# SSD stage: one running-sums matmul per head, diagonal blocks clipped by ScalarE, z and values in two PSUM banks each

## The reference

```python
proj = h @ w_in[i]
z, xbc, dt_raw, q_a, kv_a, k_rope_raw, gates = jnp.split(proj, [...], axis=-1)
...
dt = jax.nn.softplus(dt_raw + dt_bias)
a = -jnp.exp(a_log)
# y_t = sum_{s<=t} (C_t . B_s) exp(sum_{s<k<=t} a_k) x_s dt_s
y = ssd_chunked_scan(xs * dt[..., None], dt * a, bm, cm)
y = y + xs * d_skip[:, None]
y = y.reshape(b, l, D_INNER) * jax.nn.silu(z)
```

## Time and profile before

| | us |
|---|---|
| median of 3 runs | 1741.97 (1741.3 to 1747.82) |
| the profiled execution | 1743.19 |
| its span | 1741.4 |
| PE busy in the span | 1678.2 |
| ACT busy in the span | 739.3 |
| DVE busy in the span | 1092.7 |

### The profile page before, as it was taken

How to read it: one execution, slowest core, us unless ns; L and a number is a source line. 1 busy time by engine, 2 the same in 40 slices (tenths; PEclk the granted TensorE clock), 3 DMA queues, 4 the chain that set the end, 5 groups by cost and what they waited for, 6 DMA issues and landing times.

```text
span 1741.4 us, 19963 instructions
## 1 busy us (share of the span) xinstructions
PE 1678.2 (96%) x7783; PEld 1326.5 (76%) x7783; DVE 1092.7 (63%) x1397; ACT 739.3 (42%) x1040; POOL 65.8 (4%) x90
## 2 busy tenths in 40 slices
PE   5999989999999999998999999998999999999998
PEld 2888767888888887885666788875668888888887
DVE  3788856532454567876767855546868796652364
ACT  3433413221222245558776323537842354441241
POOL 0005000000000000000000000001310000000000
PEclk9999998999999999999999999998999999999999
DMA  9454321222222232221111222220012222222222
GB/s 383 173 197 171 121 94 56 97 97 98 95 96 98 97 141 73 97 97 49 49 49 53 75 93 93 89 99 25 1 64 106 97 97 97 97 97 97 97 97 97
DMA packets 25422, 174.18 MB, mean 100 GB/s; under 512 B 2800, under 2 KB 3184, under 8 KB 5104
## 3 DMA queue, kind: packets, MB, share of 16 engines
q1 hardware_dynamic: 21440, 146.52, 23.5%
q10 hardware_dynamic: 3888, 26.38, 3.8%
HBM read 168.69 MB, written 4.19 MB: 99 GB/s over the span
## 4 chain that ended last, share of the span: by engine, by line
PE 79%; DVE 11%; ACT 6%; issue 2%; DMA 2%; ACTq 0%; DVEq 0%
PE bank L1512 24%; PE bank L1514 24%; PE bank L1513 24%; ACT p L378 2%; DVE w_lo L852 2%; DMA ada_chunk<-ada 2%; ACT pt L378 1%; DVE p L1260 1%; PE bank L2022 1%; PE bank L1877 1%; PE bank L1711 1%; PE bank L1693 1%; DVE rs_g L1284 1%; PE bank L1997 1%; ACT w_hi L378 1%
## 5 line engine op out<-in xcount | busy, mean ns | idle before, releaser
L1512 PE MATMUL bank<-h,w_hi 128*128 128x512 f32 x1200 | 478.3, 399 | 15.0 <-DVE zt L1226 5.0
L1514 PE MATMUL bank<-h,w_lo 128*128 128x512 f32 x1200 | 471.2, 393 | 0.0
L1513 PE MATMUL bank<-h,w_hi 128*128 128x512 f32 x1200 | 471.0, 393 | 0.0
L378 ACT ACTIVATE w_hi<-raw 128x2048 fp32r<-128x2048 f32 (+1 forms) x129 | 246.5, 1911 | 333.6 <-DMA raw<-slabs 329.2
L852 DVE TENSOR_TENSOR w_lo<-raw,w_hi 128x2048 fp32r<-128x2048 f32 (+1 forms) x129 | 294.6, 2284 | 103.0 <-ACT w_hi L378 99.2
L1512 PEld LDWEIGHTS bank<-h,w_hi 128*128 128x128 f32 x1200 | 227.7, 190 | 67.5 <-issue 18.4
L1513 PEld LDWEIGHTS bank<-h,w_hi 128*128 128x128 f32 x1200 | 227.6, 190 | 47.8 <-issue 1.2
L1514 PEld LDWEIGHTS bank<-h,w_lo 128*128 128x128 f32 x1200 | 227.5, 190 | 47.8
L1512 PE MATMUL bank<-a_hi,w_hi 128*128 128x512 f32 x432 | 168.4, 390 | 1.7 <-DVE a_lo L858 1.7
L1514 PE MATMUL bank<-a_hi,w_lo 128*128 128x512 f32 x432 | 168.3, 390 | 0.0
L1513 PE MATMUL bank<-a_lo,w_hi 128*128 128x512 f32 x432 | 168.3, 390 | 0.0
(11 more groups left out here) (340 smaller groups left out, 2264.0 us busy)
## 6 DMA issues: line engine op xcount, KB each, us to landing
raw<-slabs SPq DMA_DIRECT2D x127, 1024.0 KB, 4.8
ada_chunk<-ada ACTq DMA_DIRECT2D x24, 1024.0 KB, 7.3
x<-x_in SPq DMA_DIRECT2D x4, 1024.0 KB, 8.8
spill_x<-x SPq DMA_DIRECT2D x1, 2048.0 KB, 12.0
x<-spill_x SPq DMA_DIRECT2D x2, 1024.0 KB, 6.6
out<-x SPq DMA_DIRECT2D x8, 256.0 KB, 2.0
raw<-slabs SPq DMA_DIRECT2D x2, 768.0 KB, 4.3
inv<-inv ACTq DMA_DIRECT2D x1, 1024.0 KB, 6.9
```

Of the source, the lines that this page charges most:

```text
L378: return act.activation(out, in_, f, **kw)
L1512: pe.matmul(out, w[0], a[0], start=start, stop=False)
L1513: pe.matmul(out, w[0], a[1], start=False, stop=False)
L1514: return pe.matmul(out, w[1], a[0], start=False, stop=stop)
```

## The change

- `running_sums` issues one matmul a head, over all 512 columns, into one bank (3 or 4). The mask matmul and its wait for the mask ahead of the stage are gone. It waits for a new signal `row_used` instead of `e2_made`; `row_used` is told when ACT has read the bank for the last time.
- ACT writes, in the place of the four exponentials of the diagonal blocks, the positive part of acum_s - acum_t (Relu with scale -1 and the new column `acum_col` as bias). The other three exponentials read the same bank. Then two more activations take exp(-value) in place in `p2`, each over two diagonal blocks of 128 columns. Above the diagonals this gives 1, and `sm` is zero there. The wait for the buffer `p2[hd % 4]` is one wait for a whole earlier pair's values instead of one for each block row.
- `acum_col` is copied once from bank 4, at xbc tile 3, into memory that the spill of x has freed.
- z alternates between banks 0 and 5, the values between 6 and 7. z tiles wait for the gate two pairs back, values for `ys_made` two pairs back. The wait of the values for `s2_taken` is as it was.
- The first group's scores come behind z tile 0, not ahead of the first running sums.

The diff, whole:

```diff
--- before.py
+++ after.py
@@ -178,6 +178,7 @@
     acum = at("acum", [S], f32, A + 97 * K)
     acum_parts = at("acum_parts", [S], f32r, A + 103 * K)
     nac_col = at("nac_col", [TOK, SSD_H], f32, A + 105 * K)
+    acum_col = at("acum_col", [TOK, SSD_H], f32, 15 * K)
     dt_col = at("dt_col", [TOK, SSD_H], f32, A + 105 * K + 512)
     rope = at("rope", [2, TOK, ROPE // 2], f32, A + 105 * K)
     qk_g = at("qk_g", [2, QK], f32, A + 104 * K)
@@ -301,7 +302,7 @@
 
     up_banks = [(first_banks, banks[0:2], banks[6:8])[n % 3] for n in range(SLABS["upa"])] + [banks[0:2]] * SLABS["upb"]
 
-    near_banks, far_banks = [banks[n] for n in (5, 7)], [banks[n] for n in (3, 4)]
+    sum_banks, z_banks, value_banks = [banks[n] for n in (3, 4)], [banks[n] for n in (0, 5)], [banks[n] for n in (6, 7)]
 
     unit_banks = [(banks[0], banks[1]), (banks[4], banks[5])]
 
@@ -635,6 +636,8 @@
                     act.wait_ge(sem("dt_turned"), 1)
                     for first, place in ((0, nac_col), (P, dt_col)):
                         do(fn(place[:], banks[4][:, first:first + P].rearrange("p (t g) -> p t g", t=TOK), ACT.Copy))
+                    act.wait_ge(sem("x_spilled"), 16)
+                    do(fn(acum_col[:], banks[4][:, 0:P].rearrange("p (t g) -> p t g", t=TOK), ACT.Copy, scale=-1.0))
                     do.tell(fn(kr_col[:], banks[7][:].rearrange("p (t g) -> p t g", t=TOK)[:, :, 64:64 + ROPE], ACT.Copy),
                             "dt_col_ready", 1)
             def half_tanh(pair):
@@ -642,24 +645,27 @@
                 if pair:
 
                     act.wait_ge(sem("z_used"), pair)
-                do.tell(fn(zt[:], banks[0][:], ACT.Tanh, scale=0.5), "z_tanh", pair + 1)
+                do.tell(fn(zt[:], z_banks[pair % 2][:], ACT.Tanh, scale=0.5), "z_tanh", pair + 1)
 
             def exponentials(hd):
                 act.wait_ge(sem("bc2_done"), hd + 1)
-                e2, shift = p2[hd % 4], nac_col[:, :, hd:hd + 1]
+                e2, total = p2[hd % 4], sum_banks[hd % 2]
                 if hd == 2:
                     act.wait_ge(sem("x_spilled"), 16)
-                for nth, (j, lo, hi, used) in enumerate(paired(0)):
-                    if hd >= 4:
-
-                        act.wait_ge(sem("pv2_done"), TOK * (hd // 2 - 2) + nth + 1)
-                    do(fn(e2[:, used:used + P], near_banks[hd % 2][:, lo:lo + P], ACT.Exp, bias=shift[:, j, :]))
+                if hd >= 4:
+
+                    act.wait_ge(sem("pv2_done"), TOK * (hd // 2 - 1))
+                for j, lo, hi, used in paired(0):
+                    do(fn(e2[:, used:used + P], total[:, lo:lo + P], ACT.Relu, scale=-1.0, bias=acum_col[:, j, hd:hd + 1]))
                     if j < TOK - 1:
-                        ins = fn(e2[:, used + P:used + hi - lo], far_banks[hd % 2][:, lo + P:hi], ACT.Exp, bias=shift[:, j, :])
-                        if nth < TOK - 1:
+                        ins = fn(e2[:, used + P:used + hi - lo], total[:, lo + P:hi], ACT.Exp, bias=nac_col[:, j, hd:hd + 1])
+                        if j < TOK - 2:
                             do(ins)
                         else:
-                            do.tell(ins, "e2_made", hd + 1)
+                            do.tell(ins, "row_used", hd + 1)
+                two, two_more = diagonals(e2, 0)
+                do(fn(two, two, ACT.Exp, scale=-1.0))
+                do.tell(fn(two_more, two_more, ACT.Exp, scale=-1.0), "e2_made", hd + 1)
 
             def pair_square(pair):
 
@@ -1223,13 +1229,13 @@
                         dt_weighted(unit)
             def gate(pair):
                 dve.wait_ge(sem("z_tanh"), pair + 1)
-                free(dve.scalar_tensor_tensor(zt[:], zt[:], 1.0, banks[0][:], ALU.add, ALU.mult), "z", pair)
+                free(dve.scalar_tensor_tensor(zt[:], zt[:], 1.0, z_banks[pair % 2][:], ALU.add, ALU.mult), "z", pair)
 
             def gated_pair(pair):
 
                 y = xbc[:, pair, :]
                 dve.wait_ge(sem("pv2_done"), TOK * (pair + 1))
-                do.tell(dve.scalar_tensor_tensor(y, y, col("d_skip", pair), banks[6][:], ALU.mult, ALU.add), "ys_made", pair + 1)
+                do.tell(dve.scalar_tensor_tensor(y, y, col("d_skip", pair), value_banks[pair % 2][:], ALU.mult, ALU.add), "ys_made", pair + 1)
                 do.tell(dve.scalar_tensor_tensor(y, zt[:], 0.5, y, ALU.mult, ALU.mult), "z_used", pair + 1)
 
             def add_square(pair):
@@ -1829,12 +1835,9 @@
             def running_sums(hd):
                 if hd >= 2:
 
-                    pe.wait_ge(sem("e2_made"), hd - 1)
-                picked, near = pick[:, hd:hd + 1].to_broadcast([P, P]), near_banks[hd % 2]
-                pe.matmul(far_banks[hd % 2][:, P:S], picked, acum_parts[:, P:S], start=True, stop=True)
-                pe.matmul(near[:], picked, acum_parts[:], start=True, stop=False)
-                pe.matmul(near[:].rearrange("p (j t) -> p j t", j=TOK), causal16, ident16.unsqueeze(1).to_broadcast([P, TOK, P]),
-                          start=False, stop=True).then_inc(sem("bc2_done"), 1)
+                    pe.wait_ge(sem("row_used"), hd - 1)
+                pe.matmul(sum_banks[hd % 2][:], pick[:, hd:hd + 1].to_broadcast([P, P]), acum_parts[:], start=True, stop=True)\
+                  .then_inc(sem("bc2_done"), 1)
 
             def group_scores(g):
 
@@ -1857,35 +1860,34 @@
             def z_tile(pair):
                 slab, m = SLAB0["z"] + pair // 2, pair % 2
                 pe.wait_ge(sem("w_split"), slab + 1)
-                if pair:
-
-                    pe.wait_ge(sem("bank_free"), FREED["z"] + pair)
+                if pair != 1:
+
+                    pe.wait_ge(sem("bank_free"), FREED["z"] + pair - 1)
                 for k in range(KT):
-                    last = three(banks[0][:], weights(slab, KT * m + k), (h3_hi[:, k, :], h3_lo[:, k, :]), k == 0, k == KT - 1)
+                    last = three(z_banks[pair % 2][:], weights(slab, KT * m + k), (h3_hi[:, k, :], h3_lo[:, k, :]), k == 0, k == KT - 1)
                 last.then_inc(sem("tile_done"), 1)
 
             def pair_values(pair):
 
                 pe.wait_ge(sem("p2_made"), 2 * pair + 2)
-                if pair:
-
-                    pe.wait_ge(sem("ys_made"), pair)
+                if pair >= 2:
+
+                    pe.wait_ge(sem("ys_made"), pair - 1)
                 pe.wait_ge(sem("s2_taken"), 2 * min((pair + 1) // 4, SSD_G - 1) + 1)
                 for nth, (j, lo, hi, used) in enumerate(paired(0)):
                     for half in range(2):
                         hd = 2 * pair + half
-                        last = pe.matmul(banks[6][64 * half:64 * half + 64, lo:hi],
+                        last = pe.matmul(value_banks[pair % 2][64 * half:64 * half + 64, lo:hi],
                                          xdt[:, j, SSD_P * hd:SSD_P * hd + SSD_P], p2[hd % 4][:, used:used + hi - lo],
                                          start=nth == 0, stop=nth == TOK - 1)
                     last.then_inc(sem("pv2_done"), 1)
 
-            group_scores(0)
-            pe.wait_ge(sem("mask_made"), 1)
             for hd in range(2):
                 running_sums(hd)
             for pair in range(XS_T):
                 z_tile(pair)
                 if pair == 0:
+                    group_scores(0)
                     for hd in (2, 3):
                         running_sums(hd)
                 if pair % 4 == 3 and pair + 1 < XS_T:
```

## The result

The changed kernel takes 1752.41 us (median of 13 runs, 1747.48 to 1754.49) against 1743.65 for the kernel before (1740.78 to 1749.17). The ratio is 1.0045, 95% interval [1.0035, 1.0055], which is 7.8 us: slower, and clear of noise, but inside the 0.5% that the prediction called no change and gave a chance of 0.36.

A forecast was written before the change was run, and what follows sets the result against it. PE bounds the kernel before; the change moves the SSD stage's bound to ACT. Floor 1.2, boundaries 4.8 and clock 4.5 sum to +10.5: 1753.7 us profiled, 1752.5 on the median's scale, range 1745.5 to 1759.

The forecast's parts named there:

- Passes at 0.45 us, Relu at the price of the exponential: SSD stage on ACT: two added 256-column passes a head, 0.45 us each with gap; Relu 0.367 like the exponential replaced.
- other estimate: Skill's pass formula: 0.40 us for 256 columns, added passes 27.5 instead of 28.8 us, total loss 9.2.
- The bound moves to ACT, floor +1.2: SSD stage: ACT mean 10.3 us a pair against PE's 8.45; without any ACT wait the stage ends 1.2 us later.
- Boundaries, +4.8: After pairs 3, 7 and 11, values wait for the next group's score copy; ACT waits 1.6 us, three times.
- The clock, +4.5: PE standing still before values at three group boundaries brings 1.2 GHz, costing 1.5 us more each.
- The 61% on slower by more than 0.5%: Whole kernel: chance 0.61 that it measures slower by more than 8.7 us, above 1750.7.
- rival (1): SSD stage: bound moves to ACT, boundaries stall, clock stays: +6.0, 1748 us; chance 0.25.
- PE's 13 and 5 us reach nobody: SSD stage: 13 us saved on sums matmuls and 5.0 on z-bank waits count only if PE sets the end.
- rival (4): SSD stage: PE still sets the end and its 13 + 5 us are won, 1725 to 1733 us; chance 0.03.
- deciding point: For PE to set the end, ACT's 64 passes must fit into 18.8 us, 0.29 each, without boundary waits.
- After the stage, a rigid move: Behind the SSD stage: DVE's extra 2 to 3 us lateness fits its 4.16 idle, so the rest moves rigidly.
- the prediction's sign of being wrong: Wrong if passes are under 0.37, ACT has gaps in every pair, or time beyond the stage changes over 1 us.

The follow-up runs named there:

- moved wait alone: Changed kernel, but values of pairs 3, 7 and 11 no longer wait for the score copy (pairs 4, 8, 12 do): 1744.88 us, ratio 1.0006.
- tripled sums: Changed kernel with every running-sums matmul issued three times: 1759.09 us, ratio 1.0094; with the score wait also put on the next pair: 1744.53, 1.0005.
- joint passes: Changed kernel with the in-place exponentials taken once for both heads of a pair: 1745.56 us, ratio 1.0007.
- squares: Changed kernel with in-place exponentials once per pair, score wait on the next pair, and 16 squares on GpSimd instead of ScalarE: 1732.28 us, ratio 0.994.

## Why the prediction was right, and where not

The forecast of 1752.5 met 1752.41 closely, but that closeness is luck: its sum of 10.5 us was too large against the ratio's 7.8, and the median of the kernel before moved up by 1.7 to 1743.65 with more runs, which hides most of the difference. The mechanism came out as forecast, with one term mis-sized. By its steps:

- **Passes at 0.45 us, Relu at the price of the exponential.** Right: 0.417 and 0.03, and 0.367. This was the number the rest hung on, interpolated from a square and a copy with the same kind of operands. The prediction's other estimate, 0.40 and a sum of 9.2, was 17 ns a pass too low; that 9.2 is nearer to 7.8 than 10.5 comes from this error going against that of the clock.
- **The bound moves to ACT, floor +1.2.** Right, shown by the moved wait alone (+1.4 in the stage, ratio 1.0006) and by the tripled sums that cost nothing there. PE isn't far behind, though: in the last four pairs it arrives together with ACT.
- **Boundaries, +4.8.** Right: stops of 1.67, 1.67 and 3.2, together 6.5, of which 1.5 is clock. Removing the wait gave 6.8.
- **The clock, +4.5.** The term that was mis-sized: 1.5 in the profile, one boundary of three. With it the sum is 1.4 + 5.0 + 1.5 = 7.9, as measured. I had looked for a single standstill of PE in such a pair, ahead of the values. There are two, of 2.6 and 2.5 us, and the lower clock after the first falls on the z tile, where it costs nothing and, as I read it, also keeps PE from coming early to the second. For that the tripled sums speak, where the first standstill was 0.85 us, the z tile ran at full clock and all three boundaries had slow values; no run changed the first standstill alone. The row I priced it by (1.5 us) was right in size. The 61% on slower by more than 0.5% rested on this term; with 1.5 in its place the sum is 7.5, and rival (1), which had no lower clock and +6.0, missed the ratio's 7.8 by 1.8 us, the forecast by 2.7.
- **PE's 13 and 5 us reach nobody.** Right. Without the passes 16 us come out, near the 18 of rival (4), whose deciding point (passes of 0.29 us) was never near.
- **After the stage, a rigid move.** Nearly: the slab copies behind the stage all show +5.7 against before until the attention stage, and there 1.5 are added. By the letter that meets the prediction's sign of being wrong (more than 1 us beyond the stage), but the sign was too fine: the profiles above spread by 2.5 us over the same instructions. The stage ended at 963.91 and not near 968, since it began 2.3 us earlier and grew by 2.6 less than forecast.

The Trainium skill's rule to put relu on VectorE ("ScalarE: Activation LUTs", "Rules for kernel authors") was not tested, since no run moved the clipping there. That taking work off ScalarE pays is shown by the joint passes and the squares.

## What to carry to other kernels

Before work is moved from one engine to another, add up each engine's work per round of the loop. Here 9.25 against 8.5 us looked like a PE-bound stage, and 0.8 us taken from one for 1.8 put on the other turned the bound over. When banks are doubled, go through every wait on the old bank: the one for the score copy stayed on the wrong pair and cost 6.8 of the 7.8 us that the change lost. And an engine that wasn't in the picture (GpSimd, idle through the stage) may take a slow version of what the new bottleneck does fast.

## What the runs showed of the hardware

A standstill of TensorE of 2.5 to 2.7 us was followed by the 1.2 GHz clock in some places and not in others of one execution (changed kernel). Of three of 3.0 us with the joint passes two were, and all three of 3.6 us with the tripled sums. Where it falls decides its price: on a z tile that nobody waited for nothing, on the values 1.1 to 2.2 us in each place. Hence work put ahead of a wait can cost more than its own time (tripled sums: 0.46 us more between values and ACT's start, and a stop behind pair 3 that is 3.1 us longer), and useless matmuls in a wait can give time back (5 us for 36 of them). The in-place pass took 416 to 420 ns each time, whether its two blocks of 128 columns lay apart (32 passes) or side by side (32 passes).
